# Pool map weights asked for in a group's third tile, and half of the key transfers issued by ScalarE

## What is computed

```python
proj = rmsnorm(x, norm_mix) @ w_in
# group B: four channel groups of 256 channels, trailing means over 2/4/8/16 positions
for gi, win in enumerate(POOL_WINDOWS):
    d = (hi - lo) / cnt - u[:, :, sl]
    outs.append(einsum('btc,cd->btd', d, pool_w[gi]))     # pool_w: (4, 256, 256)
o_b = concatenate(outs) * pool_scale * silu(z_B)
x = x + concatenate([o_a, o_b]) @ w_out
# cross-attention of the sample tokens reads cached memory keys
scores = einsum('bthd,bmhd->bhtm', qx, cache_mem_k)       # 8 requests x 256 keys x 2048
```

## Time and profile before

| | us |
|---|---|
| median of 3 runs (1671.69 to 1671.94) | 1671.75 |
| the profiled execution | 1671.06 |
| its span (the rest lies around it) | 1669.3 |
| PE busy | 1624.9 (97%) |
| DVE busy | 985.9 (59%) |
| ACT busy | 655.2 (39%) |
| POOL busy | 182.3 (11%) |

### The profile page before, as it was taken

One profiled execution on the slowest core, in us unless ns is written; L12 is line 12 of the kernel. 1 busy time (PEld: TensorE's weight loads), 2 busy tenths in 40 slices (PEclk: granted clock), 3 DMA queues, 4 the chain that ended last, 5 costly groups with the idle time before them and its releaser, 6 DMA issues.

```text
span 1669.3 us, 31335 instructions
## 1 busy us (share of the span) xinstructions
PE 1624.9 (97%) x12650; PEld 1503.6 (90%) x12650; DVE 985.9 (59%) x1689; ACT 655.2 (39%) x1115; POOL 182.3 (11%) x191
## 2 busy tenths in 40 slices
PE   7999999999999999999998889999999999899998
PEld 5887899999999999999998889999999995499998
DVE  5676446665756747655453454344588753389942
ACT  5666345254442543434322122222334322234542
POOL 0121001111121112111100001111100000001120
PEclk9999999999999999999999989999999999999999
DMA  7898734243232432333499974777313359953462
GB/s 265 254 297 250 220 93 119 57 108 101 71 96 53 114 91 76 91 94 85 102 207 211 210 179 138 222 226 222 116 55 99 101 214 418 376 156 104 128 182 107
DMA packets 320670, 263.35 MB, mean 158 GB/s; under 512 B 15049, under 2 KB 287314, under 8 KB 315234
## 3 DMA queue, kind: packets, MB, share of 16 engines
q1 hardware_dynamic: 320320, 261.99, 53.7%
q10 hardware_dynamic: 258, 0.09, 0.0%
HBM read 218.09 MB, written 44.30 MB: 157 GB/s over the span
## 4 chain that ended last, share of the span: by engine, by line
PE 81%; SPq 6%; DVE 5%; DMA 4%; issue 2%; ACT 1%; POOL 0%; ACTq 0%; DVEq 0%; POOLq 0%
PE pj L288 41%; PE pj L487 10%; PE pj L2292 7%; PE dk L2292 5%; DMA kin<-in_cache_mem_k_dram 3%; PE pj L3046 2%; SPq L1652 2%; PE dk L2556 2%; PE pj L2589 1%; DMA values_raw_b<-in_cache_mem_v_dram 1%; DVE kout L1656 1%; PE dk L1273 1%; PE pj L2567 1%; SPq L1646 1%; PE dk L1279 1%
## 5 line engine op out<-in xcount | busy, mean ns | idle before, releaser
L288 PE MATMUL pj<-a_hi,w_high 128*128 128x272 f32 x1792 | 394.0, 301 | 0.0
L288 PE MATMUL pj<-a_hi,w_low 128*128 128x272 f32 x1792 | 370.2, 288 | 0.0
L288 PE MATMUL pj<-a_lo,w_high 128*128 128x272 f32 x1792 | 369.6, 288 | 0.0
L288 PEld LDWEIGHTS pj<-a_hi,w_high 128*128 128x128 f32 x1792 | 280.8, 189 | 13.4 <-issue 8.1
L288 PEld LDWEIGHTS pj<-a_lo,w_high 128*128 128x128 f32 x1792 | 281.6, 188 | 0.0
L288 PEld LDWEIGHTS pj<-a_hi,w_low 128*128 128x128 f32 x1792 | 280.1, 189 | 0.1
L272 DVE TENSOR_TENSOR w_low<-w_raw,w_high 128x2048 fp32r<-128x2048 f32 x76 | 173.9, 2288 | 139.4 <-ACT w_high L262 139.4
L262 ACT ACTIVATE w_high<-w_raw 128x2048 fp32r<-128x2048 f32 x76 | 145.4, 1913 | 58.3 <-PE pj L288 45.9
L288 PE MATMUL pj<-mix_hi,w_high 128*128 128x272 f32 x512 | 107.2, 291 | 2.1 <-issue 2.1
L288 PE MATMUL pj<-mix_lo,w_high 128*128 128x272 f32 x512 | 106.7, 290 | 0.0
L2176 ACT ACTIVATE q_high<-q_part 128x512 fp32r<-128x512 f32 x140 | 77.5, 621 | 73.9 <-DVE q_part L2230 35.2
(11 more groups left out here) (468 smaller groups left out, 2980.3 us busy)
## 6 DMA issues: line engine op xcount, KB each, us to landing
w_raw<-in_w_in_dram SPq DMA_DIRECT2D x48, 1024.0 KB, 6.0
w_raw_wide<-in_w_ck_dram SPq DMA_DIRECT2D x16, 1024.0 KB, 8.9
w_raw_wide<-in_w_cv_dram SPq DMA_DIRECT2D x16, 1024.0 KB, 7.9
w_raw<-in_w_out_dram SPq DMA_DIRECT2D x16, 1024.0 KB, 6.2
q_part<-in_w_cq_dram SPq DMA_DIRECT2D x48, 256.0 KB, 3.6
kin<-in_cache_mem_k_dram SPq DMA_DIRECT2D x40, 256.0 KB, 5.8
keysT_scratch<-kout SPq DMA_DIRECT2D x80, 128.0 KB, 2.4
w_raw<-in_w_co_dram SPq DMA_DIRECT2D x8, 1024.0 KB, 6.3
```

The lines of the kernel that those rows point to most:

```text
L288: mm = pe.matmul(pj[:, 2 * (q % 2) + b, 0:n], wt[:, k, :], x(k, o, n), start=(k == 0 and m == 0), stop=(k == KT - 1 and m == 2))
```

## The change

Four edits:

1. `pw`: `sp_map(g)` asks for group g's weights, after the wait on `pooled`, in the third tile (q = 2) of group g itself; for g = 0, in the first tile of group 1, ahead of `sp_ust`. The request in `sp_out` goes away.
2. The keys of the pool stage: SP issues the DMAs of quadrants 0 and 1 (`SP_QUARTERS`), ACT those of quadrants 2 and 3 (`ACT_QUARTERS`). SP does so at the place where it did before; ACT at the end of the tile's part of its program, behind the read of the tile's product. Both wait for both transposes. Counts of semaphores and sizes of transfers stay.
3. The same for the out stage, in `act_out`, whose loop is written out for that.
4. The first `t_cast` of the cq stage waits until all late keys are stored.

```diff
+        SP_QUARTERS, ACT_QUARTERS = (0, 1), (2, 3)
+
+        def load_units(sp, n, quarters):
             if 0 < n <= POOL_UNITS:
                 sp.wait_ge(k_turned.sem, k_turned.at(2 * n))
                 for f in range(2):
-                    keys_out(sp, kout[f], (n - 1) // 2, 8 * ((n - 1) % 2) + f, 2, 0, 4, k_stored[f])
+                    keys_out(sp, kout[f], (n - 1) // 2, 8 * ((n - 1) % 2) + f, 2, 0, 4, k_stored[f], quarters)
...
+        def sp_map(sp, g):
+
+            at_least(sp, pooled, g)
+            for k in range(2):
+                sp.dma_start(pw[:, k], t["pool_w"][0, g, k * P:(k + 1) * P, :].rearrange("c (d n) -> c d n", d=2)).then_inc(pw_loaded, 16)
...
                         if not first:
+                            if g == 1:
+                                sp.wait_ge(oa_done, HEADS)
+                                sp_map(sp, 0)
                             sp_ust(sp, g - 1, 1)
-                            at_least(sp, oa_done, HEADS)
-                            at_least(sp, pooled, g - 1)
-                            for k in range(2):
-                                sp.dma_start(pw[:, k], t["pool_w"][0, bass.ds(g - 1, 1), k * P:(k + 1) * P, :].rearrange(
-                                    "o c (d n) -> c (o d) n", d=2)).then_inc(pw_loaded, 16)
+                    if q == 2 and not first:
+                        sp_map(sp, g)
                     if q == 3:
                         sp_ust(sp, g, 0)
                     if not first:
-                        sp_keys(sp, 4 * (g - 1) + q)
+                        load_units(sp, 4 * (g - 1) + q, SP_QUARTERS)
...
                         act.activation(halves(mixo[:, 8 + 2 * g + q, :]), product(q), ACT.Silu).then_inc(pj_read, 1)
+                        if g > 0:
+                            load_units(act, 4 * (g - 1) + q, ACT_QUARTERS)
                         continue
...
                     act.activation(sqx[:], x2[q % 2][:], ACT.Square).then_inc(sqx_ready, 1)
-            body(0)
-            with act.Fori(1, 4) as j:
+                    load_late_units(act, i, ACT_QUARTERS)
+            for j in range(4):
                 body(j)
...
             act.wait_ge(S.t_step.sem, S.t_step.at(4 * idx + 4))
+            if S is CQ and idx == 0:
+                for s in k_late_stored:
+                    act.wait_ge(s.sem, s.at(64 * OUT_UNITS))
```

More of the change, by code:

```diff
@@ L1639, in build, with keys_in, keys_out @@
         k_late_turned = Reused(conv_step, 9 * HEADS + 2 * POOL_UNITS)
-        def keys_in(sp, dst, b, first, loaded):
-            for i in range(4):
+        def keys_in(eng, dst, b, first, loaded, quarters):
+            for i in quarters:
                 cols = slice(first + i * dst.shape[-1], first + (i + 1) * dst.shape[-1])
                 src = t["cache_mem_k"][0, b].rearrange("(g m) h d -> m g (h d)", m=T32)
-                sp.dma_start(dst[i * T32:(i + 1) * T32], src[:, :, cols]).then_inc(loaded.sem, 16)
-        def keys_out(sp, src, b, tile, step, first, n, stored):
-            for i in range(4):
+                eng.dma_start(dst[i * T32:(i + 1) * T32], src[:, :, cols]).then_inc(loaded.sem, 16)
+        def keys_out(eng, src, b, tile, step, first, n, stored, quarters):
+            for i in quarters:
                 dst = keysT_d[b, first * T32:(first + n) * T32, tile + step * i, :].rearrange("(j d) m -> d j m", d=T32)
-                sp.dma_start(dst, src[i * T32:(i + 1) * T32].rearrange("p j g m -> p j (g m)")).then_inc(stored.sem, 16)
+                eng.dma_start(dst, src[i * T32:(i + 1) * T32].rearrange("p j g m -> p j (g m)")).then_inc(stored.sem, 16)
         def keys_turn(dve, dst, src):
             return dve.transpose(dst[:].rearrange("p j g m -> p g j m"), src.rearrange("p g (j d) -> p g j d", d=T32))
-        def sp_keys(sp, n):
+        SP_QUARTERS, ACT_QUARTERS = (0, 1), (2, 3)
+        def load_units(sp, n, quarters):
             if 0 < n <= POOL_UNITS:
@@ L1666, in sp_keys @@
                     sp.wait_ge(oa_done, HEADS)
-                keys_in(sp, kin, n // 2, 8 * P * (n % 2), k_in_loaded)
+                keys_in(sp, kin, n // 2, 8 * P * (n % 2), k_in_loaded, quarters)
         def dve_keys(dve, n):
@@ L1924, in build, with load_late_units @@
         assert C_INCL + 2 * MEM <= C_INV
-        def sp_keys_late(sp, i):
+        def load_late_units(sp, i, quarters):
             if 1 < i <= OUT_UNITS + 1:
@@ L1931, in sp_keys_late @@
                 for f in range(2):
-                    keys_out(sp, kout_late[f], b, 4 * h, 1, 2 * f, 2, k_late_stored[f])
+                    keys_out(sp, kout_late[f], b, 4 * h, 1, 2 * f, 2, k_late_stored[f], quarters)
             if 0 < i <= OUT_UNITS:
@@ L1936, in sp_keys_late @@
                 b, h = divmod(2 * POOL_UNITS + i - 1, XH)
-                keys_in(sp, kin_late, b, h * XD, k_late_loaded)
+                keys_in(sp, kin_late, b, h * XD, k_late_loaded, quarters)
         def dve_keys_late(dve, i):
@@ L1959, in body @@
                     if is_first(j) and q == 0:
[L1960 to L1963, removed]
                         sp_ust(sp, NG - 1, 1)
@@ L1970, in body @@
                         sp_x2(sp, j if q else j - 1, (q - 1) % 4)
-                    sp_keys_late(sp, 4 * j + q)
+                    load_late_units(sp, 4 * j + q, SP_QUARTERS)
             body(0)
```

## The result

| | before | after |
|---|---|---|
| median (5 runs each), us | 1671.75 | 1656.13 |
| lowest to highest, us | 1667.0 to 1671.9 | 1655.5 to 1660.6 |
| the profiled execution, us | 1671.06 | 1655.45 |
| its span, us | 1669.3 | 1653.6 |

The ratio is 0.9916, with a 95% interval of 0.9904 to 0.9929: 14 us faster by the ratio, 15.6 by the medians. The changed kernel ran once more on another chip: 1655.87 us and 0.9911 (0.9886 to 0.9937).

A forecast was written before the change was run, and what follows sets the result against it. Two limits side by side: PE with its stops for `pw`, and the key loop. PE's `ux` step moves from 997.48 to 979.9, 17.6 us earlier; 1671.06 - 17.6 = 1653.5, plus 0.7 for the median, 1654 us; range 1650 to 1664.

The forecast's parts named there:

- Part 1: Pool stage maps: requesting `pw` earlier removes PE's three stops and the slow maps behind, minus 16.9 us for PE alone.
- Part 2: Pool stage key loop: two queues shorten the period per unit from 15.1 to 13.3 us, transfers keeping their rates.
- part 4: ACT's added issues: covered in the pool stage by 0.6 us; out stage has 5.8 us to spare, issues take 2.6.
- The ground given for 13.3: Key loop period: 4.0 stores + 5.2 loads + 1.7 other + 2.4 transposes, each transfer kind at its own rate.
- both halves: Rival: key loads gain from writing both partition halves, period 12.2, 1652.4 us; chance 0.29, plus 0.03 if the clock stays up.
- Part 3: End of pool stage: last unit's first store to PE's `ux` step takes 17.5 us instead of 19.3.
- The start: Pool stage: ACT can start key unit 1 at 842.7, once it has read its tile.
- ACT's issues are dear: Rival, out stage and key loop: costly ACT DMA issues, a loss from about 0.97 us each; 1699 us at 1.2; chance 0.06.
- Nothing: Rival: DMA engines limit the key loop, second queue gives nothing; period 15.1, 1.4 us won, 1670.4 us; chance 0.08.

The follow-up runs named there:

- the other pairs: The changed kernel with SP on quadrants 0 and 2 and ACT on 1 and 3, in both stages: 1671.34 us, ratio 1.0009 to the kernel before.
- the kernel with loads alone: The changed kernel with all eight key stores of a pool unit in SP's queue, ACT issuing only two loads: 1650.45 us, ratio 0.9884 to the kernel before.
- The cast-first run: The changed kernel with ACT's six key DMAs of a pool unit behind the next weight cast instead of ahead: 1654.43 us, ratio 0.9899 to the kernel before.

## Why the prediction came out right, step by step

The forecast was 1654 us, the measurement 1656.1: right in sign, in size and in the mechanism, with three terms off that partly cancel, and one argument that was incomplete. That the start came early took 2.1 us of the 4.4 by which the period and the tail were too short; so part of the closeness is luck.

**Part 1 held.** No stop for `pw`, maps of 3.7 to 3.9 us, clock 1.00 through the stage. Alone it gave 5.5 us of its 16.9 by the ratio, since the gate at the end kept the rest, as the prediction said it would.

**Part 2: the period was 13.61 us, forecast 13.3.** Nine periods make 2.8 us more. The transfers came out as summed: from a unit's first store to its last load's landing 11.1 us (mean of eight), forecast 13.3 - 2.4 = 10.9, before 12.8. The mis-sized term is **ACT's issues**: priced at 0.44 us each by the earlier trace rows, 2.7 us for six, they took 4.1. The load issues had a median of 0.92 us (before 0.46), the stores about 0.5. Why is not shown: in nearly every unit both queues issued at once, but SP's second pair of the stage, at 837.88, took 1.89 us while ACT issued nothing. The longer issues made DVE's order the limit in two units with windows (14.4 us), which part 4 called covered by 0.6 us. It was not covered: PE stood 1.4 us for `w_low`. The prediction names such a stop as a sign that ACT's place in its program is the limit, and for these two units it was.

**The ground given for 13.3 was incomplete.** "Only the order of issue is sure to change" held for the change as it was made: the loads landed 4.1 us from first to last, before and after. But it would have let the other pairs run as fast. They gave 15.7 us and 1671 us, the value of the rival in which the second queue gives nothing. The Trainium skill says in "DMA: Bandwidth & Descriptors", section "Rules for kernel authors", that transfers to disjoint partition halves serialize and that a second issuing engine saves issue time only. The trace agrees for these pairs, with the 4.1 us; nothing in the rule would let the choice of pairs cost 15 us, and the measurement decides. The Trainium skill's "SBUF — State Buffer", section "Door 1: The DMA port swizzle", puts partitions 0 to 63 and 64 to 127 on different ports. That fits the sign of it; no run shows the ports themselves, and the neighbours in DRAM are an untested rival. The prediction's rival "both halves" wanted loads that move faster (4.0 instead of 5.2 us), and they did not. Its remark that no row of before has two such loads at once is also wrong: before, the four loads were issued within 2.0 us and landed 4.7 to 7.0 us after their issue, so all four were under way together (905.02 to 913.5).

**Part 3: the tail was 19.1 us, forecast 17.5.** I shortened it by 1.8 us, as ACT issues four stores instead of eight. ACT was indeed ready at 967.5, 4.4 us behind its first store, but the last store took 4.38 us to land where it had taken 2.67, with the weight block and the other queue's stores beside it. `mix_hi` waited for the landing, 5.9 us behind the first store (before 6.1). The last store was issued 1.9 us earlier in the unit, and it landed only 0.2 us earlier.

**The start** was 2.1 us early: 840.59 instead of 842.7. Of this 1.3 us are an offset that was there when the stage began (its first SiLU at 824.68 instead of 825.95), and 0.6 the fact that ACT's DMA issue began with the read in front of it, not behind it. So 979.9 became 979.9 - 2.1 + 2.8 + 1.6 = 982.2, the measured step. PE's waits at the end were 6.8 us, forecast 4.4.

**Part 4, out stage:** the issues took mostly 0.8 to 1.1 us a pair there (at most 1.5), the cast of the first full unit began at 1025.45, and PE had no stop. Held, and the run with the late keys back in SP's queue shows that nothing clear of 3 us was to be had either.

**The rivals.** "ACT's issues are dear" had its threshold at 0.97 us for all six DMAs of an out tile. There ACT's loads, of half the size, took 0.50 us (median) and its stores 0.45, so it was far off. In the pool stage the loads reached a median of 0.92 us, the stores did not, and it stayed at the small stop. "Nothing" gave the numbers of the kernel with the other pairs.

## What to carry to other kernels

When a stop is removed beside a second loop, ask which event gates the end of the stage, and whether one turn of that loop can stand in the next stage: moving one unit was worth at least as much as doubling its queues. When a second queue is to help, try it with the other kind of transfer (loads beside stores) and with few DMAs; where both queues carry the same kind at once, try which blocks they ask for together, here each queue on its own half of the partitions. And ask what the second queue's own program makes it wait for: here a tile's read, and through it every stop of PE. Price an issue by rows of transfers of the same size in the same traffic, and a tail by the landing of its last transfer, not by its issue.

## What the runs showed of the hardware that was not expected

- In the changed kernel the issue of a 256 KB key load took 0.92 us on ACT and 0.93 on SP (medians from 836 to 965 us), with one queue 0.46. In the kernel with loads alone ACT's two took 0.86 us together while SP issued stores, 0.43 each. The 128 KB loads of the out stage took 0.50 us on ACT and 0.46 on SP.
- The same DMAs in two queues took 13.6 or 15.7 us a unit, by which quadrants of 32 partitions the two queues asked for at the same moment (237 or 207 GB/s over 98 us). With stores in one queue and the loads staggered, the pairs made no difference (246 and 247 GB/s).
- An issue of ACT began at the same moment as the ACTIVATE in front of it in the program (below), while the next ACTIVATE, the cast, waited until 844.19, when the issues had ended:

```profile
840.59 0.62 ACT L1754 ACTIVATE mixo<-pj 128x544 f32<-128x544 f32 x1 [13.02 <-PE pj L288]
840.59 1.59 ACTq L1652 DMA_DIRECT2D keysT_scratch<-kout  x3
```

- What stays open: why the other pairs are slower (partition halves or neighbours in DRAM, stores or loads), why the load issues doubled, and how much of the 0.3 us a unit between the changed kernel and the one with loads alone comes from the overlap of reads and writes and how much from ACT's shorter issues. The cast-first run, where ACT's issue time delays no cast of the same tile, kept 13.6 us, which speaks for the overlap but doesn't prove it.
